# Gathering an expert's tokens: one-hot columns stationary and 512 token columns moving, then transposes, in place of 48 narrow matmuls

## The chip, the cores and the metric

The kernel runs on one core of a Trainium2 chip. The metric is the device time of one execution in microseconds, the median of several runs. The engines are named as the profile names them: PE is the matrix engine (PEld its weight loads), DVE the vector engine, ACT the scalar engine, POOL the GpSimd engine, SP the engine that issues most DMAs.

## What is computed

Two layers of a streaming encoder run over 288 tokens, 256 of a prompt and 32 of a later stream. A layer is a norm, a token-mixing part and a channel-mixing part. The first layer's channel mixing is one dense SwiGLU. The second layer's takes the two best of eight SwiGLU experts for each token:

```python
for e in range(N_EXPERTS):
    out = out + w_e[..., e:e + 1] * swiglu(h, e_gate[j, e], e_up[j, e], e_down[j, e])
```

With D_MODEL 1024 and 3584 hidden columns an expert, w_e is zero for all but two experts of a token. The change is in this part alone.

## The kernel before

Activations lie channel-major: h holds 8 blocks of 128 channels by 288 tokens. For the experts, PE also turns h token-major (L899), in three blocks of 128, 128 and 32 tokens (BLK), and ACT and DVE split it into a high and a low fp32r part, h_tm_hi and h_tm_lo. Everything that the experts multiply is split like this: high times high, high times low and low times high are summed in PSUM, so that fp32r matmuls reach nearly fp32 accuracy.

Each expert works on at most 128 of its tokens (CAP). The matrix G (L1859, DVE, three blocks) is one-hot: G[token, slot] is 1 where the token has that slot. `gather` (L915 to L924) picks the expert's tokens from h_tm with it and leaves them channel-major in hg_hi and hg_lo, which have two halves, for this expert and the next. It works in four parts p: parts 0 and 2 for the high half, 1 and 3 for the low one, parts 0 and 1 for channels 0 to 511, 2 and 3 for the rest. A part is 12 matmuls: for each of four channel blocks, three token blocks are summed; 128 x 128 token values are the stationary side and G's 128 columns the moving one. A part fills one PSUM bank, and ACT copies it out (L1348). For the first expert DVE copies the low parts (L1875).

The weights come as units of 128 x 2048 values, 1 MB each, through seven slots; the queue SP issues the load of a unit when PE has finished the unit seven before it (unit_done). ACT makes a unit's high part (`high`, L1355, four buffers), DVE the low part in place (`low`, L1871). An expert has 14 pairs of 256 hidden columns (j from 0 to 13), each with two gate/up units and one down unit. PE's order in a pair, written out by hand in `expert`, is: the gate/up unit w = 0 of the next pair (L946, L948, L951, four matmuls of 512 columns each), the turn of this pair's activations (L959, two transposes), sometimes one extra piece, the gate/up unit w = 1, and the down unit (L971, L972, L977). The extra pieces are: two scatters of the result of the expert before (pairs 1 to 4), the selection matrix (pair 5, L936), and one part of the gather for the next expert in each of the pairs 8 to 11:

```python
if p == 0:
    pe.wait_ge(s["route_made"], it + h + 2)
    pe.wait_ge(s["sel_made"], it + h + 1)
if p == 1 and not first:
    pe.wait_ge(s["moe_added"], m0 + 8 * h + 8)
if p == 3:
    pe.wait_ge(s["hghi_made"], 2 * it + 2 * h + 3)
gather(p, (7, other, other + 1, 7)[p])
```

In pair 13 the gate/up units are already the next expert's, and wait for hg_hi and hg_lo. ACT's order in a pair is: high, the turned activations (L1364), high, then the copy of the gather's part, silu (L1360), high. DVE's is: low, the low part of the turned activations (L1886), low, the product (`mult`, L1881), additions to x (pairs 1 to 4), low. The first expert has nothing ahead of it: its gather's four parts run back to back, then the gate/up units start.

Of the kernel before, what the change touches and what calls it, by code (L numbers as in the profile page):

```python
# [25 lines left out]
F32 = mybir.dt.float32  # L26
# [7 lines left out]
P = 128  # L34
D = 1024
# [81 lines left out]
def build(nc, a, o):  # L117
    with ExitStack() as ctx:
# [54 lines left out]
        with ExitStack() as experts_only:  # L173
            with ExitStack() as same_place:
                unit6_r = same_place.enter_context(nc.sbuf_tensor("unit6_r", [P, UNIT], F32R))
            (unit6, his_, hg_hi, hg_lo, htm_hi, htm_lo, yhi, ylo, G_, Sel, eh_hi, eh_lo, egate, eact, wcol, wslot,
             rall_) = (
                experts_only.enter_context(nc.sbuf_tensor(name, [P, cols], dt))
                for name, cols, dt in (
                    ("unit6", UNIT, F32), ("unit_hi", HIS * UNIT, F32R), ("hg_hi", 2 * KD * CAP, F32R),  # L180
                    ("hg_lo", 2 * KD * CAP, F32R), ("h_tm_hi", 3 * D, F32R), ("h_tm_lo", 3 * D, F32R),
                    ("y_hi", D, F32R), ("y_lo", D, F32R), ("G", 3 * CAP, F32R), ("Sel", T, F32R),
# [283 lines left out]
        def _(pe):  # L466
# [416 lines left out]
            def experts():  # L883
# [32 lines left out]
                def gather(p, bank):  # L916

                    src = htm_lo if p % 2 else htm_hi
                    for k in range(4):
                        for b, (t0, nt) in enumerate(BLK):  # L920
                            c0 = 512 * (p // 2) + 128 * k
                            i = mm(ps[:, bank, CAP * k:CAP * k + CAP], src[0:nt, b, c0:c0 + 128], G[0:nt, b, :],  # L922
                                   start=(b == 0), stop=(b == 2))
                    i.then_inc(s["hg_full"], 1)  # L924
# [56 lines left out]
                def expert(it2, h, first, last):  # L981
# [10 lines left out]
                    for j in range(PAIRS):  # L992
# [20 lines left out]
                        if not last and 8 <= j <= 11:  # L1013
                            p = j - 8
                            if p == 0:
                                pe.wait_ge(s["route_made"], it + h + 2)
                                pe.wait_ge(s["sel_made"], it + h + 1)
                            if p == 1 and not first:
                                pe.wait_ge(s["moe_added"], m0 + 8 * h + 8)
                            if p == 3:  # L1020
                                pe.wait_ge(s["hghi_made"], 2 * it + 2 * h + 3)
                            gather(p, (7, other, other + 1, 7)[p])
# [11 lines left out]
                for p in range(4):  # L1034
                    gather(p, 3 + p)
# [80 lines left out]
        def _(act):  # L1116
# [217 lines left out]
            def experts():  # L1334
# [10 lines left out]
                def gathered(number, hp, p, bank):  # L1345
                    act.wait_ge(s["hg_full"], number)
                    part = slice(4 * (p // 2), 4 * (p // 2) + 4)
                    fn((hg_lo if p % 2 else hg_hi)[:, hp, part], ps[:, bank, :].rearrange("p (k c) -> p k c", k=4),  # L1348
# [97 lines left out]
        def _(dve):  # L1446
# [406 lines left out]
            def experts():  # L1853
# [39 lines left out]
                def expert(it2, h, first, last):  # L1893
# [3 lines left out]
                    for j in range(PAIRS):  # L1897
# [26 lines left out]
                        if more:  # L1924
                            low(u0, q + 4)
# [245 lines left out]
```

## Time and profile before

| what | us |
|---|---|
| median of three runs | 2176.72 |
| the three runs | 2172.87, 2176.72, 2177.47 |
| the profiled execution | 2173.31 |
| its span, first to last instruction | 2171.5 |
| PE busy in the span | 2080.8 |
| DVE busy | 1413.3 |
| ACT busy | 1021.1 |
| POOL busy | 140.4 |

The execution that was profiled took 2173.31 us, 1.8 more than the span in which its instructions lie; the times of rows are counted from the start of the span. The experts begin at about 1083 us and fill the second half. A busy PE says that matmuls were in flight, not that each ran at full rate: they overlap, so their cost is read from the distance between starts, not from the length of one.

### The profile page before, as it was taken

The numbers are of one execution on the slowest core, as the hardware profiler recorded it, in microseconds if no ns is written. First come the engines' busy times: TensorE is split into PE (matmuls) and PEld (weight loads), VectorE is DVE, ScalarE is ACT, GpSimd is POOL, SyncE is SP. The second block draws the span as 40 slices with busy tenths as digits, with TensorE's granted clock in tenths as the row PEclk, the third lists the DMA queues.
The fourth block names the chain that finished last, engine by engine and source line by source line (L and its number), as shares of the span: only waits on it lengthen the run. The fifth ranks groups of instructions, "written<-read, shape, count | busy, mean of one in ns | idle before, by whom it ended". The sixth has DMA issues, their size and how long they took to land.

```text
span 2171.5 us, 27716 instructions
## 1 busy us (share of the span) xinstructions
PE 2080.8 (96%) x10564; PEld 1688.0 (78%) x10564; DVE 1413.3 (65%) x1736; ACT 1021.1 (47%) x1168; POOL 140.4 (6%) x108
## 2 busy tenths in 40 slices
PE   7999998899999999997899999999999999999998
PEld 5767685699997777785778888888887888888886
DVE  1445633377772447433368787978878788797887
ACT  1333311143332334211256666766666666676765
POOL 2000000154430000000000000000000000000000
PEclk9999998999999999998889999999999999999999
DMA  7312210424443322110469897988979889898895
GB/s 278 123 64 117 88 48 17 161 101 162 174 161 119 120 106 88 59 59 17 154 227 341 320 343 299 360 321 336 344 268 356 322 335 344 305 353 327 330 349 214
DMA packets 61584, 467.41 MB, mean 215 GB/s; under 512 B 7592, under 2 KB 7848, under 8 KB 9744
## 3 DMA queue, kind: packets, MB, share of 16 engines
q1 hardware_dynamic: 58896, 459.86, 56.0%
q0 software_dynamic: 2560, 5.85, 0.8%
q8 instruction: 80, 1.31, 0.2%
q14 instruction: 48, 0.39, 0.0%
HBM read 462.66 MB, written 3.02 MB: 214 GB/s over the span
## 4 chain that ended last, share of the span: by engine, by line
PE 92%; DVE 5%; ACT 2%; issue 1%; POOL 0%; DMA 0%; DVEq 0%; ACTq 0%; POOLq 0%
PE ps L501 12%; PE ps L946 10%; PE ps L951 10%; PE ps L948 9%; PE ps L646 8%; PE ps L971 5%; PE ps L977 5%; PE ps L972 5%; PE ps L922 4%; PE ps L665 3%; PE ps L842 2%; PE ps L846 2%; PE ps L849 2%; PE ps L959 1%; PE ps L865 1%; PE ps L866 1%
## 5 line engine op out<-in xcount | busy, mean ns | idle before, releaser
L1871 DVE TENSOR_TENSOR ring_r<-ring,unit_hi 128x2048 fp32r<-128x2048 f32 x288 | 653.0, 2290 | 134.2 <-ACT unit_hi L1355 131.9
L1355 ACT ACTIVATE unit_hi<-ring 128x2048 fp32r<-128x2048 f32 x288 | 542.6, 1913 | 3.4 <-issue 3.4
L946 PE MATMUL ps<-unit_hi,hg_hi 128*128 128x512 f32 x896 | 251.2, 402 | 2.3 <-issue 2.3
L948 PE MATMUL ps<-unit_hi,hg_lo 128*128 128x512 f32 x896 | 242.2, 392 | 0.0
L646 PE MATMUL ps<-h,ring 128*128 128x288 f32 x768 | 217.8, 423 | 1.7 <-ACT arena L1188 1.0
L501 PE MATMUL ps<-h,ring 128*128 128x288 f32 x832 | 208.6, 413 | 9.5 <-DVE h L1463 9.5
L951 PE MATMUL ps<-ring_r,hg_hi 128*128 128x512 f32 x772 | 212.3, 397 | 1.4 <-issue 1.4
L501 PEld LDWEIGHTS ps<-h,ring 128*128 128x128 f32 x832 | 160.4, 193 | 56.1 <-issue 11.4
L948 PEld LDWEIGHTS ps<-unit_hi,hg_lo 128*128 128x128 f32 x896 | 169.3, 189 | 37.2
L946 PEld LDWEIGHTS ps<-unit_hi,hg_hi 128*128 128x128 f32 x896 | 160.7, 189 | 34.2 <-issue 2.8
L971 PE MATMUL ps<-unit_hi,h_e_hi 128*128 128x512 f32 x448 | 178.2, 398 | 3.2 <-DVE h_e_lo L1886 3.2
L972 PE MATMUL ps<-unit_hi,h_e_lo 128*128 128x512 f32 x448 | 176.1, 393 | 0.0
L646 PEld LDWEIGHTS ps<-h,ring 128*128 128x128 f32 x768 | 142.3, 195 | 41.3 <-issue 3.8
L951 PEld LDWEIGHTS ps<-ring_r,hg_hi 128*128 128x128 f32 x772 | 145.3, 188 | 35.6 <-issue 1.7
L1364 ACT ACTIVATE h_e_hi<-ps 128x256 fp32r<-128x256 f32 x112 | 43.1, 385 | 197.4 <-PE ps L959 197.4
L1871 DVE TENSOR_TENSOR unit_r<-unit,unit_hi 128x2048 fp32r<-128x2048 f32 x48 | 109.9, 2290 | 18.5 <-ACT unit_hi L1355 17.3
L425 POOL TENSOR_TENSOR w_lo<-ring,w_hi 128x1024 fp32r<-128x1024 f32 x44 | 107.8, 2451 | 127.5 <-ACT w_hi L1294 127.4
L1360 ACT ACTIVATE e_gate<-ps 128x256 f32<-128x256 f32 x112 | 43.2, 386 | 139.8 <-PE ps L951 139.8
L977 PE MATMUL ps<-ring_r,h_e_hi 128*128 128x512 f32 x380 | 104.0, 395 | 0.0
L971 PEld LDWEIGHTS ps<-unit_hi,h_e_hi 128*128 128x128 f32 x448 | 84.2, 188 | 24.6 <-issue 5.6
L1762 DVE TENSOR_TENSOR x<-x,ps 128x288 f32<-128x288 f32 x176 | 70.9, 454 | 43.5 <-PE ps L867 43.4
L972 PEld LDWEIGHTS ps<-unit_hi,h_e_lo 128*128 128x128 f32 x448 | 84.3, 188 | 17.9
(383 smaller groups left out, 2889.1 us busy)
## 6 DMA issues: line engine op xcount, KB each, us to landing
ring<-in_w_exp SPq DMA_DIRECT2D x288, 1024.0 KB, 4.8
ring<-in_w_mix SPq DMA_DIRECT2D x44, 1536.0 KB, 6.6
unit<-in_w_exp SPq DMA_DIRECT2D x48, 1024.0 KB, 4.8
ring<-in_w_ffn SPq DMA_DIRECT2D x22, 1536.0 KB, 6.3
rel_table<-rel_row POOLq DMA_DIRECT2D x8, 256.0 KB, 8.9
const<-in_const SPq DMA_DIRECT2D x1, 1186.0 KB, 8.6
x<-in_xT SPq DMA_DIRECT2D x1, 1152.0 KB, 5.1
out_yT<-x SPq DMA_DIRECT2D x4, 288.0 KB, 2.2
```

The costliest lines, as they stand in the source:

```text
L425: nc.gpsimd.tensor_tensor(w_lo[:, r], slot[:, (MIX + i) % RING, q, :], w_hi[:, r].bitcast(F32), ALU.subtract).then_inc(s["gu_lo_made"], 1)
L501: i = mm(ps[:, bank, 0:T], w[:, k, :], src[:, k], start=(k == 0), stop=(k == KD - 1))
L646: i = mm(ps[:, 0, 0:T], w[:, k, :], h[:, k], start=(k == 0), stop=(k == KD - 1))
L922: i = mm(ps[:, bank, CAP * k:CAP * k + CAP], src[0:nt, b, c0:c0 + 128], G[0:nt, b, :], start=(b == 0), stop=(b == 2))
L946: mm(out, hg_hi[:, hp, 4 * w + k, :], hi[:, 512 * k:512 * k + 512], start=(w == 0 and k == 0), stop=False)
L948: mm(out, hg_lo[:, hp, 4 * w + k, :], hi[:, 512 * k:512 * k + 512], start=False, stop=False)
L951: z = mm(out, hg_hi[:, hp, 4 * w + k, :], lo[:, 512 * k:512 * k + 512], start=False, stop=(w == 1 and k == 3))
L971: mm(out, eh_hi[:, c], hi[:, cols], start=(j == 0 and c == 0), stop=False)
L972: mm(out, eh_lo[:, c], hi[:, cols], start=False, stop=False)
L977: z = mm(ps[0:CAP, 3 + 2 * h + half, :], eh_hi[:, c], lo[:, cols], start=False, stop=(j == PAIRS - 1 and c == 1))
L1355: fn(unit_hi(q), unit(q), ACT.Copy).then_inc(s["uhi_made"], 1)
L1871: v.tensor_tensor(unit_lo(q), unit(q), unit_hi(q).bitcast(F32), ALU.subtract).then_inc(s["ulo_made"], 1)
```

## The change

The tokens are gathered token-major first and turned afterwards. `gather(w, bank)` now has G as the stationary side and 512 columns of h_tm_hi or h_tm_lo as the moving one: for each half w of the channels, six matmuls (three token blocks, high and low part) sum into one bank, with a slot's token in each row. ACT copies the bank into a new fp32 buffer, hg_tm (`gathered`). `turn_tokens(w, bank)` turns four blocks of 128 columns of it with fp32 transposes into one bank; from there ACT writes the high part to hg_hi (`tokens_high`), and DVE subtracts it from the bank to give hg_lo (`tokens_low`).

In an expert, pairs 8 and 9 hold the two gathers, pairs 10 and 11 the two turns. The wait for sel_made, which frees bank 7, moves from pair 8 to pair 10, and that for moe_added from pair 9 to pair 8; the turns wait for hgtm_made. hg_tm takes the place of the buffer y_hi, which other pairs use. For the first expert both gathers, both turns and the gate/up units follow each other, each behind its own wait.

```diff
-                def gather(p, bank):
-                    src = htm_lo if p % 2 else htm_hi
+                def gather(w, bank):
+                    for b, (t0, nt) in enumerate(BLK):
+                        for src in (htm_hi, htm_lo):
+                            i = mm(ps[0:CAP, bank, :], G[0:nt, b, :], src[0:nt, b, 512 * w:512 * w + 512],
+                                   start=(b == 0 and src is htm_hi), stop=(b == 2 and src is htm_lo))
+                    i.then_inc(s["hg_full"], 1)
+                def turn_tokens(w, bank):
                     for k in range(4):
-                        for b, (t0, nt) in enumerate(BLK):
-                            c0 = 512 * (p // 2) + 128 * k
-                            i = mm(ps[:, bank, CAP * k:CAP * k + CAP], src[0:nt, b, c0:c0 + 128], G[0:nt, b, :],
-                                   start=(b == 0), stop=(b == 2))
-                    i.then_inc(s["hg_full"], 1)
+                        i = nc.tensor.transpose(ps[:, bank, CAP * k:CAP * k + CAP],
+                                                hg_tm[0:CAP, 512 * w + 128 * k:512 * w + 128 * k + 128], ident[0:CAP, 0:CAP])
+                    i.then_inc(s["hgT_full"], 1)
...
                         if not last and 8 <= j <= 11:
-                            p = j - 8
-                            if p == 0:
+                            w = j % 2
+                            if j == 8:
                                 pe.wait_ge(s["route_made"], it + h + 2)
+                                if not first:
+                                    pe.wait_ge(s["moe_added"], m0 + 8 * h + 8)
+                            if j == 10:
                                 pe.wait_ge(s["sel_made"], it + h + 1)
-                            if p == 1 and not first:
-                                pe.wait_ge(s["moe_added"], m0 + 8 * h + 8)
-                            if p == 3:
-                                pe.wait_ge(s["hghi_made"], 2 * it + 2 * h + 3)
-                            gather(p, (7, other, other + 1, 7)[p])
+                            if j < 10:
+                                gather(w, other + w)
+                            else:
+                                pe.wait_ge(s["hgtm_made"], 2 * it + 2 * h + 3 + w)
+                                turn_tokens(w, (7, other)[w])
...
-                for p in range(4):
-                    gather(p, 3 + p)
+                for w in range(2):
+                    gather(w, 3 + w)
+                for w in range(2):
+                    pe.wait_ge(s["hgtm_made"], w + 1)
+                    turn_tokens(w, 5 + w)
...
-                def gathered(number, hp, p, bank):
+                def gathered(number, w, bank):
                     act.wait_ge(s["hg_full"], number)
-                    part = slice(4 * (p // 2), 4 * (p // 2) + 4)
-                    fn((hg_lo if p % 2 else hg_hi)[:, hp, part], ps[:, bank, :].rearrange("p (k c) -> p k c", k=4),
-                       ACT.Copy).then_inc(s["hglo_made" if p % 2 else "hghi_made"], 1)
+                    fn(hg_tm[0:CAP, 512 * w:512 * w + 512], ps[0:CAP, bank, :], ACT.Copy).then_inc(s["hgtm_made"], 1)
+                def tokens_high(number, hp, w, bank):
+                    act.wait_ge(s["hgT_full"], number)
+                    fn(hg_hi[:, hp, 4 * w:4 * w + 4], ps[:, bank, :].rearrange("p (k c) -> p k c", k=4), ACT.Copy) \
+                        .then_inc(s["hghi_made"], 1)
...
-                def gathered(number, half, bank):
-                    dve.wait_ge(s["hg_full"], number)
-                    v.tensor_copy(hg_lo[:, 0, 4 * half:4 * half + 4], ps[:, bank, :].rearrange("p (k c) -> p k c", k=4)) \
-                        .then_inc(s["hglo_made"], 1)
+                def tokens_low(number, hp, w, bank):
+                    dve.wait_ge(s["hghi_made"], number)
+                    part = slice(4 * w, 4 * w + 4)
+                    v.tensor_tensor(hg_lo[:, hp, part], ps[:, bank, :].rearrange("p (k c) -> p k c", k=4),
+                                    hg_hi[:, hp, part].bitcast(F32), ALU.subtract).then_inc(s["hglo_made"], 1)
...
+                        if not last and 10 <= j <= 11:
+                            w = j % 2
+                            tokens_low(2 * it + 2 * h + 3 + w, 1 - h, w, (7, other)[w])
                         if more:
                             low(u0, q + 4)
```

The order on PE ahead of the first expert. Before, from the ranks of the tokens (L913) over the four parts (L922) to the first gate/up matmuls (L946):

```order
L913 MATMUL ps<-small_route,const 128x8 x3
L922 MATMUL ps<-G,h_tm_hi 128x128 x12
L922 MATMUL ps<-G,h_tm_lo 128x128 x12
L922 MATMUL ps<-G,h_tm_hi 128x128 x12
L922 MATMUL ps<-G,h_tm_lo 128x128 x12
L946 MATMUL ps<-unit_hi,hg_hi 128x512 x4
```

With the change, the end of the same place; the last two of twelve matmuls of 512 columns (L921), then eight transposes (L928) and the first gate/up unit (L952, L954, L957):

```order
L921 MATMUL ps<-h_tm_hi,G 128x512
L921 MATMUL ps<-h_tm_lo,G 128x512
L928 MATMUL ps<-const,hg_tm 128x128 x8
L952 MATMUL ps<-unit_hi,hg_hi 128x512 x4
L954 MATMUL ps<-unit_hi,hg_lo 128x512 x4
L957 MATMUL ps<-ring_r,hg_hi 128x512 x4
```

The four groups of twelve have become one of twelve wide matmuls and one of eight transposes, still all ahead of the first gate/up unit.

The order on PE in an expert, from a turn to the next gate/up unit. Before, in pair 8:

```order
L959 MATMUL ps<-const,e_act 128x128 x2
L922 MATMUL ps<-G,h_tm_hi 128x128 x12
L946 MATMUL ps<-unit_hi,hg_hi 128x512 x4
L948 MATMUL ps<-unit_hi,hg_lo 128x512 x4
L951 MATMUL ps<-unit_r,hg_hi 128x512 x4
```

With the change, the end of pair 8, where the last two of six gather matmuls (L921) stand ahead of the gate/up unit (L952 and on), and then pair 10, with the turn (L965) and the four transposes of gathered tokens (L928):

```order
L921 MATMUL ps<-h_tm_hi,G 128x512
L921 MATMUL ps<-h_tm_lo,G 128x512
L952 MATMUL ps<-unit_hi,hg_hi 128x512 x4
L954 MATMUL ps<-unit_hi,hg_lo 128x512 x4
L957 MATMUL ps<-unit_r,hg_hi 128x512 x4
```

```order
L957 MATMUL ps<-ring_r,hg_hi 128x512 x4
L965 MATMUL ps<-const,e_act 128x128 x2
L928 MATMUL ps<-const,hg_tm 128x128 x4
L952 MATMUL ps<-unit_hi,hg_hi 128x512 x4
L954 MATMUL ps<-unit_hi,hg_lo 128x512 x4
L957 MATMUL ps<-ring_r,hg_hi 128x512 x4
```

One group of twelve narrow matmuls after the turn has become six wide ones in pairs 8 and 9 and four transposes in pairs 10 and 11; what stands around them is as before.

The order on DVE in pair 10 and into pair 11 of a loop's first expert, from the low part of a unit over the product (e_act) and two more low parts to the low part of the turned activations (h_e_lo). Before:

```order
L1871 TENSOR_TENSOR ring_r<-ring,unit_hi 128x2048
L1881 TENSOR_TENSOR e_act<-e_gate,ps 128x256
L1871 TENSOR_TENSOR ring_r<-ring,unit_hi 128x2048
L1871 TENSOR_TENSOR ring_r<-ring,unit_hi 128x2048
L1886 TENSOR_TENSOR h_e_lo<-ps,h_e_hi 128x256
```

With the change:

```order
L1891 TENSOR_TENSOR ring_r<-ring,unit_hi 128x2048
L1902 TENSOR_TENSOR e_act<-e_gate,ps 128x256
L1896 TENSOR_TENSOR hg_lo<-ps,hg_hi 128x512
L1891 TENSOR_TENSOR ring_r<-ring,unit_hi 128x2048
L1891 TENSOR_TENSOR ring_r<-ring,unit_hi 128x2048
L1907 TENSOR_TENSOR h_e_lo<-ps,h_e_hi 128x256
```

The subtraction that gives hg_lo now stands behind the product and ahead of the low parts of the last unit of this pair and the first of the next.

## Rows read from the trace of the kernel before

**Rows 1.** The page's part 4, the chain that ended last, by engine.

```profile
PE 92%; DVE 5%; ACT 2%; issue 1%; POOL 0%; DMA 0%; DVEq 0%; ACTq 0%; POOLq 0%
```

**Rows 2.** Busy us by stretch, two experts: engines, clock, DMA share, GB/s.

```profile
1241.71:1374.89 133.18, 133.18 (x606) 107.96 (x605) 109.53 (x86) 90.47 (x77) 0.00 (x0) 1.00 0.85 323
1374.89:1508.06 133.17, 133.17 (x606) 107.95 (x605) 109.55 (x86) 90.56 (x77) 0.00 (x0) 1.00 0.90 339
```

**Rows 3.** Waits of PE from 1110 us on: total us, times, longest.

```profile
PE ps L971 <- DVE h_e_lo L1886: 3.2, 2, 2.0
PE ps L946 <- issue: 2.3, 1, 2.3
```

**Rows 4.** Line L922's weight loads, one a matmul, ns min/median/max; h_tm_lo's row reads alike.

```profile
L922 PEld LDWEIGHTS ps<-G,h_tm_hi x192: 181/186/333, 1082.9 to 2009.4; 128*128 128x128 f32 x128, 32*128 32x128 f32 x64
```

**Rows 5.** Timeline of PE, turns and one gate/up unit: start us, us.

```profile
1602.10 0.38 PE L959 MATMUL ps<-const,e_act 128*128 128x128 f32 x2
...
1610.35 1.09 PE L946 MATMUL ps<-unit_hi,hg_hi 128*128 128x512 f32 x4
...
1613.14 0.38 PE L959 MATMUL ps<-const,e_act 128*128 128x128 f32 x2
...
1624.15 0.38 PE L959 MATMUL ps<-const,e_act 128*128 128x128 f32 x2
...
1632.68 0.38 PE L959 MATMUL ps<-const,e_act 128*128 128x128 f32 x2
```

**Rows 6.** Timeline of PE, narrow windows: a turn's second transpose; the selection's three.

```profile
1613.25 0.27 PE L959 MATMUL ps<-const,e_act 128*128 128x128 f32 x1
...
1553.29 0.56 PE L936 MATMUL ps<-const,G 128*128 128x128 f32 x3
```

**Rows 7.** Lines L1348 and L1811, copies and subtractions out of PSUM: ns min/median/max.

```profile
L1348 ACT ACTIVATE hg_hi<-ps x16: 597/600/602, 1087.1 to 2009.8; 128x512 fp32r<-128x512 f32 x16
...
L1811 DVE TENSOR_TENSOR h_tm_lo<-ps,h_tm_hi x6: 669/680/691, 1077.8 to 1080.8; 128x512 fp32r<-128x512 f32 x4, 32x512 fp32r<-32x512 f32 x2
```

**Rows 8.** Timeline around the first expert's gather, all engines.

```profile
1082.91 4.12 PE L922 MATMUL ps<-G,h_tm_hi 128*128 128x128 f32 x12 [1.83 <-DVE G L1859]
...
1086.47 0.20 ACT L1397 ACTIVATE small<-const 128x1 f32<-128x1 f32 x1
...
1099.20 2.07 PE L946 MATMUL ps<-unit_hi,hg_hi 128*128 128x512 f32 x4
1099.31 0.69 DVE L1875 CAST hg_lo<-ps 128x512 fp32r<-128x512 f32 x1 [7.47 <-PE ps L922]
...
1105.98 2.27 DVE L1871 TENSOR_TENSOR ring_r<-ring,unit_hi 128x2048 fp32r<-128x2048 f32 x1
...
1108.30 0.77 PEld L951 LDWEIGHTS ps<-ring_r,hg_hi 128*128 128x128 f32 x4 [0.41 <-DVE ring_r L1871]
```

**Rows 9.** Stretches of PE: us, busy (instructions), granted clock, DMA share, GB/s; last row all engines.

```profile
1074.60:1078.40 3.80, 3.80 (x18) 0.50 0.00 0
1078.60:1081.80 3.20, 2.48 (x25) 1.00 0.01 3
1082.00:1099.00 17.00, 16.09 (x48) 0.50 0.00 1
1099.20:1102.30 3.10, 3.10 (x8) 0.50 0.00 0
...
1641.80:1645.00 3.20, 3.20 (x8) 2.31 (x7) 0.93 (x1) 1.57 (x1) 0.00 (x0) 0.50 1.01 412
```

**Rows 10.** Timeline of PE in that last stretch, gate/up matmuls at half clock.

```profile
1642.24 1.91 PE L948 MATMUL ps<-unit_hi,hg_lo 128*128 128x512 f32 x4
1643.94 1.05 PE L951 MATMUL ps<-ring_r,hg_hi 128*128 128x512 f32 x2
```

**Rows 11.** The last expert: a pair's stretch, and unit loads with us from issue to landing.

```profile
2114.60:2123.10 8.50, 8.50 (x40) 6.91 (x38) 7.41 (x6) 6.16 (x6) 0.00 (x0) 1.00 0.99 374
...
ring<-in_w_exp SPq DMA_DIRECT2D x13, 1024.0 KB, 4.8
```

More of the change, by code:

```diff
@@ L175, in build @@
                 unit6_r = same_place.enter_context(nc.sbuf_tensor("unit6_r", [P, UNIT], F32R))
-            (unit6, his_, hg_hi, hg_lo, htm_hi, htm_lo, yhi, ylo, G_, Sel, eh_hi, eh_lo, egate, eact, wcol, wslot,
+                yhi = same_place.enter_context(nc.sbuf_tensor("y_hi", [P, D], F32R))
+            (unit6, hg_tm, his_, hg_hi, hg_lo, htm_hi, htm_lo, ylo, G_, Sel, eh_hi, eh_lo, egate, eact, wcol, wslot,
              rall_) = (
@@ L179, in build @@
                 for name, cols, dt in (
-                    ("unit6", UNIT, F32), ("unit_hi", HIS * UNIT, F32R), ("hg_hi", 2 * KD * CAP, F32R),
+                    ("unit6", UNIT, F32), ("hg_tm", D, F32), ("unit_hi", HIS * UNIT, F32R), ("hg_hi", 2 * KD * CAP, F32R),
                     ("hg_lo", 2 * KD * CAP, F32R), ("h_tm_hi", 3 * D, F32R), ("h_tm_lo", 3 * D, F32R),
-                    ("y_hi", D, F32R), ("y_lo", D, F32R), ("G", 3 * CAP, F32R), ("Sel", T, F32R),
+                    ("y_lo", D, F32R), ("G", 3 * CAP, F32R), ("Sel", T, F32R),
                     ("h_e_hi", 2 * P, F32R), ("h_e_lo", 2 * P, F32R), ("e_gate", 2 * P, F32), ("e_act", 2 * P, F32),
@@ L1387, in expert @@
                         if not last and 8 <= j <= 11:
-                            p = j - 8
-                            gathered(4 * it + 4 * h + 4 + p + 1, 1 - h, p, (7, other, other + 1, 7)[p])
+                            w = j % 2
+                            if j < 10:
+                                gathered(2 * it + 2 * h + 3 + w, w, other + w)
+                            else:
+                                tokens_high(2 * it + 2 * h + 3 + w, 1 - h, w, (7, other)[w])
                         if not end:
@@ L1397, in experts @@
                 fn(small[:, 40:41], c_("rw", 1), ACT.Silu)
-                gathered(1, 0, 0, 3)
-                gathered(3, 0, 2, 5)
+                for w in range(2):
+                    gathered(w + 1, w, 3 + w)
+                for w in range(2):
+                    tokens_high(w + 1, 0, w, 5 + w)
                 high(0, 0, 2)
@@ L1923, in expert @@
                             add_result(m0 + 8 * h + d + 1, d, other)
+                        if not last and 10 <= j <= 11:
+                            w = j % 2
+                            tokens_low(2 * it + 2 * h + 3 + w, 1 - h, w, (7, other)[w])
                         if more:
@@ L1928, in experts @@
                 low(0, 0)
-                gathered(2, 0, 4)
-                gathered(4, 1, 6)
+                for w in range(2):
+                    tokens_low(w + 1, 0, w, 5 + w)
                 low(0, 1)
```

## Prediction

> **What bounds the kernel now.** I read the page's chain of waits first: TensorE (PE) carries 92% of what ended last [rows 1]. Then the experts one by one. Their stretches of 133 us repeat to a few hundredths, PE is busy in all of the 133.17 us, VectorE (DVE) in 109.5, ScalarE (ACT) in 90.5, and the DMA engines 0.85 to 0.90 of the time [rows 2]. From 1110 us on, PE waits on another engine for 3.2 us in all, twice, for DVE [rows 3]. So in the experts a microsecond of PE work is a microsecond of the kernel, as long as DVE, ACT and the weight stream keep up with a faster PE. The gather itself is 384 matmuls in two groups of 192, eight gathers of 48 [rows 4]: one ahead of the first expert, at half clock, and seven inside experts, each spread over pairs 8 to 11.
>
> **What the seven inner gathers cost now.** Every pair has one turn (L959), so PE's timeline is measured from turn to turn: pairs with a gather part take 11.04 and 11.01 us (1602.10, 1613.14, 1624.15), the next one, without, 8.53 (to 1632.68) [rows 5]. The part costs 2.51 and 2.48; I take 2.48, times four parts: **9.9 us** an expert. A matmul of 128 moving columns thus costs 0.207 us in a row.
>
> **What takes their place.** Pairs 8 and 9 now each hold six matmuls of 512 moving columns, from the same kind of tiles (fp32r on both sides). Twelve such matmuls, each with its own weight load, run from 1610.35 to 1613.14 [rows 5]: 0.2325 us each, only 12% more than one with 128 columns. So 12 x 0.2325 = 2.8 us. Pairs 10 and 11 each hold four fp32 transposes, the form that the turn has: its two start at 1613.14 and 1613.25, 0.11 us apart [rows 5, 6]. Eight of them: 0.9 us. The lower end for a transpose is 0.085: a pair without a gather is 36 x 0.2325 = 8.37 us of its 8.53, which leaves 0.16 for the two. The upper end is 0.19, three that last 0.56 us together where tokens are selected (L936) [rows 6]; I take 0.11, since that is the same form in the same surroundings. New cost 2.8 + 0.9 = 3.7 us; saved **6.2 us an expert** (6.4 to 5.6 by the ends), and seven times that is **43.4 us**.
>
> Beside the row of 0.11 us between transposes, with 0.27 us as what one alone lasts [rows 6], the Trainium skill ("TensorE: Matmul & The Clock Gate", "Part 4: PE-mode transpose") gives a transpose about 275 ns in one kernel's context. The trace agrees with that as the duration of one, not as the distance between two; taken as the price it would make the eight 2.2 us and the forecast below 9 us longer.
>
> **What lies beside PE.** ACT copies four 128 x 512 tiles out of PSUM for each gather, before and after: 0.60 us each [rows 7]; before, all four were halves of hg_hi and hg_lo, now two are hg_tm and two hg_hi. Nothing is added. DVE gains two subtractions of 128 x 512 from PSUM an expert, 0.68 us each by the same form in h_tm_lo [rows 7]: 1.4 us on 109.5, against a stretch that shrinks to 127.0. It is 87% busy then, and the new ones stand after the product of a pair, where DVE waits for ACT anyhow. I cost both at nothing. If that cover were gone, the whole 1.4 us an expert, 10 us in all, would come back. The new waits of PE are for copies queued two pairs (some 18 us) earlier, so nothing queues behind them. The wait for hg_lo moves from the copy to a subtraction in pair 11, two pairs ahead of its reader.
>
> The DMA queue issues the same units, each when PE frees its slot. An expert brings 42 units of 1.05 MB, 44 MB; in 127.0 us that is 347 GB/s. In the last expert, which has no gather, pairs at PE's full pace follow each other: 374 GB/s in such a stretch, with landings still 4.8 us after issue [rows 11]. So the stream holds this pace, and I cost it at nothing too.
>
> **The gather ahead of the first expert.** It lies alone on the path: 48 matmuls from 1082.91, the last copy on DVE at 1099.31, then the low part of unit 2 from 1105.98 (2.27 long), for which PE waits at 1108.30 [rows 8]. That chain on DVE sets the end. It begins with the last half of hg_lo, done at 1100.0. In the new order there are five links. Twelve matmuls of 512 columns: at half clock 0.425 us each (from 1642.24 to 1643.94, four of them [rows 10]), 5.1 us in all, end 1088.0; if the clock rises on the way, as it did behind the first gate/up matmuls (0.50 from 1099.2 to 1102.3 [rows 9], 1.00 in the experts [rows 2]), say for the last five, about 1087.1. ACT is free at 1086.67 (it loads a function table before) [rows 8]; two copies of 0.60, the second from 1087.3 or 1088.05. Four transposes, 0.45 to 0.75. Two more copies of 0.60 and two subtractions of 0.68, one behind the other in part. The end comes to 1089.9 (clock up) or 1090.95 (half clock), 10.1 or 9.05 us sooner than 1100.0. I take **9.6**. PE itself needs 8.7 us from its first gate/up matmul to the low part of unit 2 (1099.20 to 1108.30 less the 0.41 that it waited) [rows 8]; it can start at 1089.2 to 1090.2, when the first half of hg_lo is there, and would be ready at 1097.9 to 1098.9, while the low part comes 8.25 us behind the last half of hg_lo, at 1098.2 to 1099.2. DVE's chain still ends last, and the shift is kept whole.
>
> **Sum.** 43.4 + 9.6 = 53 us less. The profiled execution took 2173.31 us (a span of 2171.5 and 1.8 around it), so 2120.3; the median of the three runs is 2176.72, 3.4 more, which gives 2123.7. The four executions stand as two near 2173 and two near 2177; from the middle, 2175, I forecast **2122 us**. With the ends of the prices (per expert 0.2 us less or 0.6 more, in the first gather 0.5 either way) and of the runs (2 us either way) it is 2118 to 2129.
>
> **Rivals.**
> *DVE and ACT come out of their cover* (chance 0.10). The new subtraction stands ahead of the low part of the unit two further on; if PE waits there for all of it, 7 x 1.4 = 10 us come back: 2132. For it speaks that DVE is already at 109.5 of 133; against it that PE never waits for DVE there now.
> *Weight loads are not hidden under the new matmuls* (0.03). If each of the twelve paid its load of 0.19 us [rows 4] apart, the saving falls by 2.3 us an expert, 16 in all: 2138. Against it: the gate/up matmuls load weights each time and keep 0.2325.
> *The clock falls* (0.03). PE sat idle once for 2.3 us in the loop, and a stretch of 3.2 us at a clock of 0.50 followed [rows 3, 9]. Two such stretches an expert, one after each run of transposes, cost 3.2 us: 7 x 3.2 = 22 us, 2144. Against it: the 24 transposes of h (L899), under way from 1074.6 to 1078.4 at 0.50, were followed by a clock of 1.00 (1078.6 to 1081.8), while 17 us of gather matmuls of 128 columns left it at 0.50 [rows 9]. The Trainium skill (same page and section) says that the faster clock does not engage for transposes, since they do not count as a busy PE; that would be this case, and the trace speaks against it here.
> *The weight stream falls behind, and the kernel is slower* (0.03). The place is the queue's issue of a unit, which follows PE's release of the slot seven units before; today's pauses for the gather, four an expert, let the landings catch up. The point is 44 MB in 133.2 us, 331 GB/s: below that rate the experts take longer than now. At 320 GB/s an expert takes 137.6 us, 7 x 4.4 - 9.6 = 21 us more than now: 2196. At 340 it would be 129.5, a gain of 26 + 9.6: 2139. Only the stretch means of 323 to 339 GB/s [rows 2] speak for it, and those are set by PE's pace; 374 [rows 11] speaks against.
> *The change does nothing that can be measured* (0.01): the gather would have to lie under another engine, and PE's full row denies it.
>
> **How the numbers follow.** The forecast has 0.80. Its own range is 2118 to 2129; the whole range takes in the first rival's 2132 with the same 2 us for the runs, and below 4 us more, the spread of the four executions: **2114 to 2134**. The rest, 2138 and above, is left out. 0.2% is 4.4 us, about what a measurement of this kernel can tell from no change; faster by more has 0.96, within 0.01, slower 0.03.
>
> **What would show it.** Right: the pairs with six gather matmuls take 9.9 us from turn to turn, those with four transposes 9.0, an expert 127.0; ACT's copies are as many as now; DVE's two new subtractions last 0.7 and PE's waits on DVE stay near 3 us; the first gate/up matmul starts near 1090; landings stay near 4.8 us. Wrong: a PE row with idle time before the low-part matmuls of pairs 11 and 12 (DVE), a clock under 1.00 behind the transposes, landings beyond 8 us (three units of PE's pace), or transposes 0.2 us and more apart.

## The result, and the profile after

The changed kernel takes **2130.44 us**, the median of four runs (2128.73 to 2131.87); the kernel before 2177.09 in four (2172.87 to 2179.73). The ratio is 0.9784, with a 95% interval from 0.9769 to 0.9799: 46.6 us faster. The forecast was 2122, its range 2114 to 2134. The execution that was profiled took 2131.87 us, with a span of 2130.0 against 2171.5 before, so between the two traces 41.5 us are to be found. The direction and the range were right; the forecast itself was 8 us too low, and the experiments below are mostly about those 8 us.

The page after, the chain of waits by engine, against [rows 1]:

```profile
PE 90%; DVE 5%; ACT 2%; issue 1%; DMA 1%; POOL 0%; SPq 0%; DVEq 0%; ACTq 0%; POOLq 0%
```

PE still sets the end. An expert, busy us by engine, granted clock, DMA share and GB/s, against [rows 2]:

```profile
1749.08:1876.87 127.79, 127.79 (x579) 103.12 (x577) 110.54 (x88) 90.06 (x77) 0.00 (x0) 1.00 0.92 346
```

An expert has 27 PE instructions fewer in its records and takes 5.38 us less than the 133.17 of before. DVE has the two instructions more that were foreseen, and 1.0 us; ACT has the same 77. Now PE in pair 8, against [rows 5] (start, us; L965 is the turn, L921 the gather, L952 the next gate/up unit):

```profile
1302.82 0.38 PE L965 MATMUL ps<-const,e_act 128*128 128x128 f32 x2
1302.96 0.48 PE L921 MATMUL ps<-h_tm_hi,G 128*128 128x512 f32 x1
1303.27 0.39 PE L921 MATMUL ps<-h_tm_lo,G 128*128 128x512 f32 x1
1303.50 0.39 PE L921 MATMUL ps<-h_tm_hi,G 128*128 128x512 f32 x1
1303.73 0.40 PE L921 MATMUL ps<-h_tm_lo,G 128*128 128x512 f32 x1
1304.06 0.50 PE L921 MATMUL ps<-h_tm_hi,G 32*128 32x512 f32 x1
1304.40 0.39 PE L921 MATMUL ps<-h_tm_lo,G 32*128 32x512 f32 x1
1304.72 1.19 PE L952 MATMUL ps<-unit_hi,hg_hi 128*128 128x512 f32 x4
...
1313.13 0.38 PE L965 MATMUL ps<-const,e_act 128*128 128x128 f32 x2
...
1323.44 0.38 PE L965 MATMUL ps<-const,e_act 128*128 128x128 f32 x2
1323.66 0.60 PE L928 MATMUL ps<-const,hg_tm 128*128 128x128 f32 x4
...
1332.46 0.38 PE L965 MATMUL ps<-const,e_act 128*128 128x128 f32 x2
```

Pairs 8 and 9 take 10.31 us from turn to turn (9.9 was predicted), pair 10 takes 9.02 and pair 11 8.98 (9.0 predicted). The starts in the part of six are the thing to read: 0.31 for the first, close behind the turn's transposes (it is 0.32 with full rows too, below), 0.23 for the next two, where all have 128 rows, and 0.32 to 0.34 from 1303.73 on, where the third token block (32 rows) comes in and goes out. The weight loads of the same stretch say why:

```profile
1303.51 0.19 PEld L921 LDWEIGHTS ps<-h_tm_lo,G 128*128 128x128 f32 x1
1304.06 0.18 PEld L921 LDWEIGHTS ps<-h_tm_hi,G 32*128 32x128 f32 x1 [0.36 <-issue]
1304.17 0.18 PEld L921 LDWEIGHTS ps<-h_tm_lo,G 32*128 32x128 f32 x1
1304.72 0.53 PEld L952 LDWEIGHTS ps<-unit_hi,hg_hi 128*128 128x128 f32 x3 [0.37 <-issue]
```

Loads of equal row count follow each other without a gap. The first load with 32 rows, and the first with 128 rows again, stand behind an idle 0.36 us: they start with their own matmul instead of ahead of it.

The first gather, against [rows 8]:

```profile
1084.40 0.77 PE L921 MATMUL ps<-h_tm_hi,G 128*128 128x512 f32 x1 [1.79 <-DVE G L1879]
...
1090.68 1.97 PE L928 MATMUL ps<-const,hg_tm 128*128 128x128 f32 x8
1093.26 2.05 PE L952 MATMUL ps<-unit_hi,hg_hi 128*128 128x512 f32 x4 [0.61 <-issue]
...
1103.43 0.38 PE L965 MATMUL ps<-const,e_act 128*128 128x128 f32 x2
...
1108.07 0.47 PE L977 MATMUL ps<-unit_hi,h_e_hi 128*128 128x512 f32 x1 [1.44 <-DVE h_e_lo L1907]
```

From the first gather matmul to the first turn it is 19.03 us, 26.43 before. The clock in it, against [rows 9] (us, PE busy, granted clock, DMA share, GB/s):

```profile
1084.40:1090.70 6.30, 6.30 (x13) 0.50 0.00 0
...
1093.30:1096.80 3.50, 3.50 (x8) 0.50 0.02 5
1097.00:1103.00 6.00, 6.00 (x28) 0.99 0.61 208
```

PE's waits on other engines behind it, against [rows 3]:

```profile
PE ps L977 <- DVE h_e_lo L1907: 6.2, 4, 2.4
PE ps L952 <- issue: 2.4, 1, 2.4
```

Both lists leave out one wait of 1.7 us for y_lo at the very end, which is the same before and after; [rows 3] stop ahead of it.

The ledger of the two traces, each row the difference of two starts on PE:

| stretch | before | after | difference |
|---|---|---|---|
| start of the first gather | 1082.91 | 1084.40 | +1.49 |
| from there to the first turn | 26.43 | 19.03 | -7.40 |
| first pair of the first expert | 10.02 | 10.29 | +0.27 |
| seven experts with a gather | 7 x 133.17 | 7 x 127.79 | -37.7 |
| where the loop over experts jumps back, above a plain pass | 5.51 | 6.79 | +1.28 |
| one stop in the third expert's first pair | | 0.44 | +0.44 |

The sum is -41.6. The start of the first gather lies ahead of everything that the change touches, and varies from 1081.4 to 1084.8 over all the traces of this study. The medians differ by 5 us more than the two traces: the profiled execution of before was among its lowest (2173.31 beside a median of 2177.09), that of after its highest.

### The profile page after: what moved, and what is told of

Same layout as the page of the kernel before. It is cut to its first block, busy times and chain, and to the rows that moved or that the text cites. A ratio compares the mean times of both kernels' runs of the same rounds, so it can differ in the third digit from the quotient of the medians.

```text
span 2130.0 us, 27280 instructions
## 1 busy us (share of the span) xinstructions
PE 2036.5 (96%) x10340; PEld 1647.0 (77%) x10340; DVE 1420.3 (67%) x1750; ACT 1019.2 (48%) x1170; POOL 140.5 (7%) x108
## 3 DMA queue, kind: packets, MB, share of 16 engines
q8 instruction: 78, 1.28, 0.2%
## 4 chain that ended last, share of the span: by engine, by line
PE 90%; DVE 5%; ACT 2%; issue 1%; DMA 1%; POOL 0%; SPq 0%; DVEq 0%; ACTq 0%; POOLq 0%
PE ps L502 13%; PE ps L952 10%; PE ps L957 9%; PE ps L954 9%; PE ps L647 8%; PE ps L977 5%; PE ps L978 5%; PE ps L983 5%; PE ps L666 3%; PE ps L843 2%; PE ps L847 2%; PE ps L850 2%; PE ps L921 1%; PE ps L866 1%; PE ps L868 1%
## 5 line engine op out<-in xcount | busy, mean ns | idle before, releaser
L952 PE MATMUL ps<-unit_hi,hg_hi 128*128 128x512 f32 x896 | 251.1, 402 | 3.0 <-issue 3.0
L954 PE MATMUL ps<-unit_hi,hg_lo 128*128 128x512 f32 x896 | 241.7, 392 | 0.0
L502 PE MATMUL ps<-h,ring 128*128 128x288 f32 x832 | 211.4, 416 | 10.1 <-DVE h L1483 10.1
L957 PE MATMUL ps<-ring_r,hg_hi 128*128 128x512 f32 x772 | 211.8, 396 | 0.0
L954 PEld LDWEIGHTS ps<-unit_hi,hg_lo 128*128 128x128 f32 x896 | 168.8, 188 | 37.4
L952 PEld LDWEIGHTS ps<-unit_hi,hg_hi 128*128 128x128 f32 x896 | 160.7, 189 | 38.4 <-issue 8.0
L957 PEld LDWEIGHTS ps<-ring_r,hg_hi 128*128 128x128 f32 x772 | 145.1, 188 | 33.8 <-DVE ring_r L1891 0.2
L1782 DVE TENSOR_TENSOR x<-x,ps 128x288 f32<-128x288 f32 x176 | 71.0, 454 | 43.4 <-PE ps L868 43.2
```

The source lines that it names most:

```text
L502: i = mm(ps[:, bank, 0:T], w[:, k, :], src[:, k], start=(k == 0), stop=(k == KD - 1))
L952: mm(out, hg_hi[:, hp, 4 * w + k, :], hi[:, 512 * k:512 * k + 512], start=(w == 0 and k == 0), stop=False)
L954: mm(out, hg_lo[:, hp, 4 * w + k, :], hi[:, 512 * k:512 * k + 512], start=False, stop=False)
L957: z = mm(out, hg_hi[:, hp, 4 * w + k, :], lo[:, 512 * k:512 * k + 512], start=False, stop=(w == 1 and k == 3))
L1782: v.tensor_tensor(x[:, d], x[:, d], ps[:, 4 + d % 4, 0:T], ALU.add).then_inc(s["ffn_added"], 1)
```

## The experiments

The theory (A, where an expectation uses a letter): PE pulls the next weight load ahead of the matmul under way only while the number of active rows stays; each visit to the 32-row block costs extra starts, in the new gather and much more in the old one. The rivals: the wide matmuls or their loads cost that much by themselves; DVE's new subtraction costs PE; the missing microseconds lie in the first gather. In each experiment the median of runs is given where there are several, otherwise one execution.

**Full rows in the new gather.** The third block of G and of both halves of h_tm is filled with zeros to 128 rows once, and the gather multiplies all of them:

```diff
-                    for b, (t0, nt) in enumerate(BLK):
+                    for b in range(3):
...
-                            i = mm(ps[0:CAP, bank, :], G[0:nt, b, :], src[0:nt, b, 512 * w:512 * w + 512],
+                            i = mm(ps[0:CAP, bank, :], G[:, b, :], src[:, b, 512 * w:512 * w + 512],
...
+                for r0, r1 in ((32, 64), (64, 128)):
+                    for tile in (G, htm_hi, htm_lo):
+                        v.memset(tile[r0:r1, 2, :].bitcast(F32), 0.0)
```

> The third token block's rows 32 to 127 are filled with zeros once, in G and in both parts of h_tm, and the gather's matmuls take all 128 rows of each block. Theory (changing the number of active rows from 128 to 32 and back exposes a weight load: in the changed kernel's trace the six matmuls of a gather start 0.315, 0.231, 0.231, 0.327 and 0.341 us apart and the next two 0.316 and 0.339, against 0.231): a pair with a gather falls from 10.31 us by 4 x 0.1 = 0.4 to 9.9, fourteen of them 5.6 us, and the first gather, at half clock, falls by about 1.1 us; in all 6.7 us under the changed kernel's time. Rival (wide matmuls with G stationary cost 0.295 us each on average whatever the rows, from contention for the same operands): pairs stay at 10.31 us and the time is unchanged. The zeros fall into DVE's idle 5 us before routing and cost nothing in both.

It took 2122.16 us (2121.56 to 2122.72, four runs), 0.9742 of before, interval 0.9722 to 0.9761. PE in pair 8, and a whole expert:

```profile
1299.57 0.38 PE L965 MATMUL ps<-const,e_act 128*128 128x128 f32 x2
1299.70 0.48 PE L921 MATMUL ps<-h_tm_hi,G 128*128 128x512 f32 x1
1300.02 0.39 PE L921 MATMUL ps<-h_tm_lo,G 128*128 128x512 f32 x1
1300.25 0.39 PE L921 MATMUL ps<-h_tm_hi,G 128*128 128x512 f32 x1
1300.48 0.40 PE L921 MATMUL ps<-h_tm_lo,G 128*128 128x512 f32 x1
1300.72 0.39 PE L921 MATMUL ps<-h_tm_hi,G 128*128 128x512 f32 x1
1300.94 0.40 PE L921 MATMUL ps<-h_tm_lo,G 128*128 128x512 f32 x1
1301.18 1.07 PE L952 MATMUL ps<-unit_hi,hg_hi 128*128 128x512 f32 x4
...
1867.56:1994.52 126.96, 126.96 (x579) 103.45 (x578) 110.56 (x88) 90.12 (x77) 0.00 (x0) 1.00 0.93 348
```

With as many matmuls, and more rows in a third of them, the starts are even from the second on, the pair is 9.89 and the expert 126.96: the 9.9 and 127.0 that were predicted for the change itself. The loads are even too (the last two of the gather's, then the gate/up unit's):

```profile
1300.72 0.19 PEld L921 LDWEIGHTS ps<-h_tm_lo,G 128*128 128x128 f32 x1
1300.95 0.88 PEld L952 LDWEIGHTS ps<-unit_hi,hg_hi 128*128 128x128 f32 x4
```

Over the whole kernel PEld sat idle ahead of 18 of the change's gather loads, 8.9 us in all, and here ahead of one, the first (1.9 us). From gather to turn it is 17.5 us. The second execution below agrees.

**Rows alternate.** The six matmuls in the order of blocks 0, 2, 1, 0, 2, 1, high part first: four changes of row count instead of two.

```diff
+                    order = ((0, htm_hi), (2, htm_hi), (1, htm_hi), (0, htm_lo), (2, htm_lo), (1, htm_lo))
+                    for n_, (b, src) in enumerate(order):
```

> Same six matmuls a gather, in the order block 0, block 2 (32 rows), block 1 of the high part, then the same of the low part: the 32-row matmuls stand apart, so the row count changes four times in a gather and not twice. Theory (row changes expose weight loads): each change costs about 0.2 us, so a pair with a gather rises from 10.31 to about 10.7 us, fourteen of them 5.6 us, and the first gather by about 1.2 us: 6 to 7 us over the changed kernel. Rival (cost per matmul, not per change): pairs stay at 10.31 us.

2136.84 us in one execution. The pair is 10.71, from one turn to the next:

```profile
1303.66 0.38 PE L966 MATMUL ps<-const,e_act 128*128 128x128 f32 x2
1303.80 1.33 PE L922 MATMUL ps<-h_tm_hi,G 128*128 128x512 f32 x3
1304.96 1.25 PE L922 MATMUL ps<-h_tm_lo,G 128*128 128x512 f32 x3
1306.05 1.09 PE L953 MATMUL ps<-unit_hi,hg_hi 128*128 128x512 f32 x4
...
1314.37 0.38 PE L966 MATMUL ps<-const,e_act 128*128 128x128 f32 x2
```

The same six matmuls in another order cost 0.40 us more, the same 0.4 that one visit costs in the change and that full rows save. It is the change of rows, not the 32 rows.

**DVE's subtraction twice.** In pairs 10 and 11 the subtraction is made a second time, into a buffer that nobody reads.

```diff
+                    if twice:
+                        v.tensor_tensor(hg_tm[:, 512 * w:512 * w + 512].rearrange("p (k c) -> p k c", k=4),
+                                        ps[:, bank, :].rearrange("p (k c) -> p k c", k=4),
+                                        hg_hi[:, hp, part].bitcast(F32), ALU.subtract)
```

> In the experts DVE does the subtraction out of PSUM twice in each of pairs 10 and 11, the first time into a buffer that nobody reads: 0.69 us more for each, 1.4 us an expert. Theory (it lies under PE's work): the stretches of experts 5 and 6 stay at 127.8 us and PE's waits for DVE stay near 6 us in all. Rival (DVE's queue already sets PE's pace there): up to 1.4 us an expert, 129.2 us, and 10 us on the whole.

The group of added instructions (count, busy us, mean ns, idle before), and an expert:

```profile
L1897 DVE TENSOR_TENSOR hg_tm<-ps,hg_hi 128x512 f32<-128x512 f32 x14 | 9.6, 684 | 0.0
...
1750.14:1877.92 127.78, 127.78 (x579) 103.13 (x577) 111.57 (x90) 90.02 (x77) 0.00 (x0) 1.00 0.91 346
```

DVE is busy 1.0 us longer and the expert takes 127.78, as in the change: the subtraction is covered. The whole execution took 2135.39, 3.5 above the change; of that the loop's jump back has 2.5 (9.28 against 6.79) and the end behind the last turn 2.5 (15.77 against 13.27), neither in a stretch with added work; its first gather began 0.9 us sooner. In both places the clock has a part. At the jump back it was 0.50 for 6.8 us instead of 3.4, behind a longer wait of PE for DVE (3.80 us against 2.40); at the end it was 0.50 from 2120.2 to 2123.6, where the change has 1.00, behind the same wait of 2.01 us in both. Why PE waits longer at the jump back was not tried, so that there a part of the added work is not excluded.

**The old first gather.** The first expert's gather as before, the inner ones as in the change.

```diff
-                for w in range(2):
-                    gather(w, 3 + w)
-                for w in range(2):
-                    pe.wait_ge(s["hgtm_made"], w + 1)
-                    turn_tokens(w, 5 + w)
+                for p in range(4):
+                    first_gather(p, 3 + p)
```

> The gather ahead of the first expert is the old one (48 matmuls of 128 columns, channel-major, copies by ACT and DVE), those inside the experts are the new ones. Theory (the first gather gives 7.1 to 7.4 us of the gain, the seven inner ones 37.8): from the first gather matmul to the first turn it is 26.4 us again instead of 19.0, experts 5 and 6 stay at 127.8 us, the time is 7 us over the changed kernel. Rival (part of the first gather's gain is given back in the first pairs, where PE waits 1.4 us for DVE): only about 5 us over it.

2136.31 us in one execution; from the first gather matmul to the first turn:

```profile
1082.12 4.12 PE L930 MATMUL ps<-G,h_tm_hi 128*128 128x128 f32 x12 [1.70 <-DVE G L1885]
...
1108.55 0.38 PE L974 MATMUL ps<-const,e_act 128*128 128x128 f32 x2
```

These 26.43 us are those of before to the hundredth, 7.40 more than in the change, with experts of 127.78. So the two parts of the change add up: 7.4 in the first gather, 37.7 in the seven others. The whole is only 4.4 us above the change's profiled execution, near the rival's 5, but mostly for other reasons: the first gather began 2.3 us sooner in this execution, and the stop in the third expert's first pair (0.44 in the ledger) is missing. The rival's own place, the first pair, gives back 0.17.

**Before, with full rows.** The kernel before, with its 48 narrow matmuls, and nothing but the zeros and the full rows of the first experiment.

```diff
-                            i = mm(ps[:, bank, CAP * k:CAP * k + CAP], src[0:nt, b, c0:c0 + 128], G[0:nt, b, :],
+                            i = mm(ps[:, bank, CAP * k:CAP * k + CAP], src[:, b, c0:c0 + 128], G[:, b, :],
```

> The kernel before the change, its 48 narrow matmuls a gather unchanged but for the third token block, which is filled with zeros to 128 rows and taken whole. It asks what the narrow form costs without row changes: a part of twelve has four matmuls of 32 rows, eight changes. Theory A (the narrow form is dear mostly by its row changes; between two matmuls of full rows it has 0.14 us): a part falls from 2.48 to 12 x 0.14 = 1.7 us or less, the pairs from 11.01 to 10.2, an expert from 133.15 to 130 us, the time by 22 us and, at half clock, some more in the first gather. Theory B (a matmul of 128 fp32r columns costs 0.2 us by itself, and the gain is that of wide moving operands): pairs stay at 11.0 us and the time is that of the kernel before.

It took 2136.62 us (2136.31 to 2138.0, four runs), 0.9821 of before, interval 0.9801 to 0.9841. PE from turn to turn in pair 8:

```profile
1303.63 0.38 PE L959 MATMUL ps<-const,e_act 128*128 128x128 f32 x2
1303.77 1.53 PE L922 MATMUL ps<-G,h_tm_hi 128*128 128x128 f32 x12
1305.14 1.13 PE L946 MATMUL ps<-unit_hi,hg_hi 128*128 128x512 f32 x4
...
1313.48 0.38 PE L959 MATMUL ps<-const,e_act 128*128 128x128 f32 x2
```

Twelve narrow matmuls take 1.37 us here (1305.14 - 1303.77), 0.11 each, half of what was read before; the pair is 9.85, with 10.98 for pair 8 before (the 11.04 and 11.01 of [rows 5] are pairs 10 and 11, 9.90 and 9.91 here), and the expert 128.65 to 128.70. It saves 41 us by the medians, nearly as much as the change (36.7 between the two traces), and its twelve narrow matmuls take less time than the change's six wide ones with a visit to 32 rows (1304.72 - 1302.96 = 1.76), though a gather has four such parts of twelve and only two of six. The effect was larger than expected.

**The short block stacked.** The low part of the third block goes into rows 32 to 63 of the high one, with G's rows repeated there, so that one matmul does both: five of full rows in place of six.

```diff
+                    for n_, (src, b) in enumerate(((htm_hi, 0), (htm_lo, 0), (htm_hi, 1), (htm_lo, 1), (htm_hi, 2))):
+                        i = mm(ps[0:CAP, bank, :], G[:, b, :], src[:, b, 512 * w:512 * w + 512],
...
+                    i = v.tensor_scalar(G[TS:2 * TS, 2], c_("iota", CAP, TS), rpos_all[0:TS, 2, bass.ds(e, 1)], None,
```

> On top of the changed kernel: the 32 rows of the third block's high part and the 32 of its low part lie one below the other in one block of 128 rows (the rest zero), with G's rows there twice, so that a gather has five matmuls of full rows. From e1's 9.89 us a pair falls by one matmul to 9.66, an expert from 126.95 to 126.5 us, the first gather by two matmuls at half clock, 0.85 us: 4.1 us under e1, about 2118 us. DVE has one more compare of 0.2 us an expert, under PE's work. If what is left in a gather were not a cost per matmul, the pair would stay at 9.89.

2123.78 us (2118.84 to 2125.42, four runs), 0.9755 of before, interval 0.9733 to 0.9778. Pairs of 9.67, an expert of 126.49 and 16.74 us from gather to turn are as expected, 0.46 an expert below the first experiment; the whole is not. The 5 us went into one place, where the loop over experts jumps back and the engines stop (idle time and its end in brackets):

```profile
1605.33 1.17 PE L951 MATMUL ps<-unit_hi,hg_hi 128*128 128x512 f32 x4 [2.25 <-issue]
...
1613.34 2.29 DVE L1895 TENSOR_TENSOR ring_r<-ring,unit_hi 128x2048 fp32r<-128x2048 f32 x1 [8.49 <-issue]
...
1617.30 0.77 PE L976 MATMUL ps<-unit_hi,h_e_hi 128*128 128x512 f32 x1 [5.98 <-DVE h_e_lo L1911]
```

DVE stops longest, 8.49 us, and PE then waits 5.98 for it. The last pair before the jump and the first behind it cost 10.61 us more than a plain pass, 5.37 in the first experiment.

**Selection on full rows too.** As the last, and the selection matrix of pair 5 (three transposes and three matmuls of one column, with the same row changes) on full rows, with its column of weights moved to 384.

```diff
-                        nc.tensor.transpose(ps[0:CAP, 7, t0:t0 + nt], G32[0:nt, b, :], ident[0:nt, 0:nt])
+                        nc.tensor.transpose(ps[0:CAP, 7, t0:t0 + 128], G32[:, b, :], ident)
...
+                        i = mm(ps[0:CAP, 7, 384:385], G32[:, b, :], wcol[:, b:b + 1], start=(b == 0), stop=(b == 2))
```

> e6, and the selection matrix in pair 5 (three transposes of G and three matmuls with one column each) takes all 128 rows of the third block too, where it also changes from 128 to 32 rows and back, twice. If row changes cost there what they cost in the gather, 0.1 to 0.2 us each, pair 5 falls from 9.96 to 9.3 to 9.6 us, eight times 3 to 5 us; if a transpose or a matmul of one column does not pay for them, it stays.

**2115.92 us** (2114.4 to 2117.98, five runs), 0.9724 of before, interval 0.9706 to 0.9741. It lies below both kernels: each was measured against before, and its interval and that of the change (0.9769 to 0.9799) do not meet. Pair 5 from turn to turn:

```profile
1271.73 0.38 PE L964 MATMUL ps<-const,e_act 128*128 128x128 f32 x2
...
1281.26 0.38 PE L964 MATMUL ps<-const,e_act 128*128 128x128 f32 x2
```

9.53 us, 9.96 in every other kernel of this study that keeps the 32-row block there. The loop's jump back costs 4.78 in this one. Of the 8 us between it and the last kernel the selection has 3.4 (8 experts by 0.43); the jump has 5.8, and a first gather that began 0.9 later in this execution takes some of it back.

**Three of them again**, to see whether the cost of the jump back is chance: the changed kernel, full rows and the stacked block.

> The changed kernel once more, for a second trace. At the jump back in the loop of experts (between the fourth and the fifth) all engines stop for instructions; the two pairs around it took 6.8 us more than elsewhere in its first trace, 5.5 in the kernel before, 5.4 in e1, 10.6 in e6, 4.8 in e7. Theory (this belongs to the program and its place in memory): 6.8 again within 0.5. Rival (chance of each execution): anything from 5 to 10. All other stretches as before: experts 5 and 6 at 127.8 us.

> e1 once more. Theory (program): 5.4 us extra around the jump again within 0.5. Rival (chance): from 5 to 10. Experts 5 and 6 at 126.95 us in both.

> e6 once more. Theory (program): 10.6 us extra around the jump again within 0.5, so that this form loses there what it saves in the gathers. Rival (chance): from 5 to 10. Experts 5 and 6 at 126.5 us in both.

| kernel | us, one execution | jump back, above a plain pass | the first time |
|---|---|---|---|
| changed | 2128.44 | 6.82 | 6.79 |
| full rows | 2121.38 | 5.24 | 5.37 |
| stacked block | 2122.19 | 10.58 | 10.61 |

In two traced executions of each program the cost agrees to 0.13 us, which speaks against chance. One of the stacked block's four runs took 2118.84 us, 5 below the other three; it has no trace, and whether its jump back was cheaper is not known. PE's two waits at the jump back make up 4.8 us in the change, 3.3 with full rows and 8.2 in the stacked block; the rest, 2.0 to 2.4 us, goes with a granted clock of 0.50 behind them. What in a program sets the waits (where its code lies, what the engines hold at that moment) was not tried and stays open.

## Why the prediction was right, and where it was off

- *PE bounds the experts.* Right: all of an expert is PE busy before and after, and a microsecond of PE was a microsecond of the kernel. Work added to DVE alone changed nothing in an expert away from the jump back.
- *The old gather: 2.48 us a part.* The size was right, the reading of it was the mistake behind the rest. "A matmul of 128 moving columns thus costs 0.207 us in a row" took a mean over starts of three kinds. With full rows they cost 0.11; the rest was weight loads that came late at eight changes of row count a part, 0.14 us each (the four pairs of a gather take 44.03 us before and 39.56 with full rows, for 32 changes). That both forms are there (128 rows x128, 32 rows x64) stood in [rows 4], and I passed over it.
- *"So 12 x 0.2325 = 2.8 us."* **This step failed.** The price came from gate/up matmuls, which all have 128 rows, and the gather's do not. A part adds 10.31 - 8.53 = 1.78 us to its pair where 1.39 was set, 3.6 for the twelve: 0.4 us a visit to the 32 rows, 0.8 an expert, 5.8 in seven (7 x 0.83, from 127.79 and 126.96). On full rows the predicted 9.9 and 127.0 came out as they stood.
- *The eight transposes at 0.11 us.* Right: pairs 10 and 11 are 9.02 and 8.98 against 9.0 predicted.
- *ACT and DVE beside PE at nothing.* Right in the experts: as many copies, subtractions of the length foreseen, and a second one of each subtraction left the expert at 127.78. PE's waits on DVE grew from 3.2 to 6.2 us: 2.4 of it is at the loop's jump back, where there was none before, 1.44 in the first pair of the first expert (1.2 before), 0.3 in the third expert, and 2.0 in the last pair as before.
- *The weight stream.* Right: 345 to 346 GB/s against the 347 worked out, and landings unchanged:

```profile
ring<-in_w_exp SPq DMA_DIRECT2D x36, 1024.0 KB, 4.8
```

- *The first gather: 9.6 us, by its ends 9.05 to 10.1.* Too much: 7.4, less 0.27 in the pair behind. The clock stayed at 0.50 through all of it, and its twelve matmuls took 6.28 us where 5.1 had been set for half clock. With full rows they take 5.25 (1084.04 to 1089.29), so row changes have 1.0 of it, 0.13 to 0.17 us a late start. From the last matmul to the last half of hg_lo it took 3.3 us (1090.68 to 1094.01) where 2.95 had been set. "DVE's chain still ends last" did not hold either: the low part of unit 2 was done at 1102.26, and PE came to it at 1102.51 without a wait, behind first gate/up matmuls that ran at 0.50. With full rows the gather's gain is 26.43 - 17.5 = 8.9, close to the lower end. It is the same mis-sized step, but it works through the clock as well. With full rows (same columns as above) the mean over the gather is

```profile
1084.04:1091.60 7.56, 6.80 (x20) 0.61 0.01 2
```

since the clock rises from 0.50 to 1.00 between 1089.6 and 1090.0, while the transposes run, and PE then waits for DVE again (1.20 us for the low part of unit 2). What the late starts and the clock each have of the 1.5 us between 19.03 and 17.5 was not separated.
- *The sum.* 43.4 + 9.6 = 53 us were forecast between two profiled executions; 37.7 + 7.4 = 45.1 came, less 0.3 in the first pair and 3.2 in the start, the jump back and one stop. Of the 8 us between forecast and median, row changes explain 5.8 + 1.5, the second with the clock in it; the rest is within what the runs differ by. The median lies 1.4 us above the 2118 to 2129 that the ends of the prices gave. It lies in the stated range because that took in the first rival's 2132, and the first rival's mechanism did not occur: that much was luck.
- *The rivals.* DVE and ACT out of their cover: refuted by the doubled subtraction, except at the jump back, where it stays open. *Weight loads not hidden*: half right. Its mechanism is what happened, at a third of its price, and in the only place where the argument against it (the gate/up matmuls keep 0.2325) said nothing: where the row count changes. The clock falling in the experts: refuted; behind a run of transposes the granted clock is 1.00 (same columns as above):

```profile
1323.00:1327.00 4.00, 4.00 (x22) 1.00 1.02 387
```

The Trainium skill ("TensorE: Matmul & The Clock Gate", "Part 4: PE-mode transpose") says that the faster clock does not engage for transposes. In this kernel that does not show. The weight stream and "nothing that can be measured": refuted by 345 GB/s and by the result.

- *What the change was worth apart from rows.* Of the 5.38 us an expert, dropping row changes has 4.5 (133.17 to 128.67, the old gather on full rows) and the new shape 1.7 (128.67 to 126.95); the visits that it still makes take back 0.8. The reshaping gained mostly by making 2 visits to the 32-row block out of 16 (one for each channel block and part before), and zeros in a short block do away with all of them alone.

## What to carry to other kernels

Before you reshape a row of small matmuls, look whether their row counts differ: a mean distance of starts may be mostly the price of switching (0.11 us of 0.207 were the work here), and padding the short block with zeros to the rows of its neighbours may be worth as much as the rewrite. Take the price of a new instruction from rows of its own form, rows included, or bound it by what a change of form costs. Compare kernels stretch by stretch as well as by their totals: here the jump back of a loop cost 4.8 to 10.6 us by program, more than some of the edits under test.

## What the runs showed of the hardware

- A weight load is not pulled ahead when the number of active rows changes between 128 and 32, in either direction; a visit to a 32-row block (of two matmuls, or of one where rows alternate) costs 0.4 us at a granted clock of 1.00, seen by removing one (9.89 against 10.31 a pair) and by adding one (10.71). The Trainium skill ("TensorE: Matmul & The Clock Gate", "Part 3: Packing small matmuls — row/col tiling") says that a weight load is pulled ahead of matmuls in flight when its row groups do not conflict with theirs or when it goes into the background weight buffer, and lists that loads overlap only when the row groups differ. In the load rows above, loads into the same 128 rows did overlap, against that list, and here the measurement decides; whether they went into a background buffer no run shows. Loads that change between 128 rows and the first 32 of them did not overlap. Loads into row groups that share no rows were not run.
- Narrow fp32r matmuls of 128 moving columns, each with its own weight load, start 0.11 us apart on full rows at a granted clock of 1.00, half of the 0.231 of one with 512 columns.
- The clock stayed at its lower level, 0.50 (1.2 GHz), through twelve back-to-back matmuls of 512 columns and eight transposes of the first gather, until 1096.8, behind the first eight gate/up matmuls. In the four traces whose first gather has six-matmul parts with row changes it rose to 1.00 (2.4 GHz) about 13 us behind the first gather matmul; in the five whose wide matmuls all have 128 rows, 5 to 6 us behind it. The narrow matmuls on full rows kept it at 0.50 for 13 us as well, so full rows alone do not settle it.
- The stop of PE, ACT and DVE at a dynamic loop's jump back, with the half clock behind it, cost the same to 0.13 us in two executions of each of three programs, and differs by up to 5.8 us between programs whose loop bodies differ by a few instructions.
